# Two-layer hybrid trunk on one core: the first modulation in eight parts of 256 channels in place of four of 512

## The reference, cut to what matters

```python
cond = jax.nn.silu(c)                                   # one row of 2048
for layer in range(DEPTH):
    shift, scale, gate = jnp.split((cond @ w_ada[layer] + b_ada[layer])[:, None, :], 3, axis=-1)
    h = rms_norm(x, norm_g[layer]) * (1.0 + scale) + shift
    (qkv_a, z_a, beta_raw, alpha_raw, glu_in, z_b, q_c, k_c, v_c, z_c,
     q_i, k_i, w_i, gate_raw) = split_columns(h @ w_in[layer])
    ...
    a_half, b_half = jnp.split(glu_in, 2, axis=-1)
    u = causal_depthwise_conv(a_half * jax.nn.sigmoid(b_half), conv_b_w[layer]) + conv_b_b[layer]
    ...
    x = x + gate * (merged @ w_out[layer])
```

## Time and profile before

| | us |
|---|---|
| median of 3 runs | 2204.05 (2202.7 to 2205.69) |
| the profiled execution, its own time | 2206.72 |
| its span in the trace | 2204.9 |
| mean granted TensorE clock | 0.985 |
| PE busy | 2140.4 (97%) |
| POOL busy | 1664.8 (76%) |
| DVE busy | 1225.2 (56%) |

### The profile page before, as it was taken

The page is one execution under the profiler, slowest core; times in us unless marked ns, Lnnn a source line. Parts: engine busy times, 40 slices in busy tenths (PEclk is TensorE's granted clock), DMA queues, the critical chain, the costliest instruction groups (busy, mean ns, idle before and its releaser), DMA issues.

```text
span 2204.9 us, 37807 instructions
## 1 busy us (share of the span) xinstructions
PE 2140.4 (97%) x14842; PEld 1949.9 (88%) x14842; DVE 1225.2 (56%) x2153; ACT 959.7 (44%) x1056; POOL 1664.8 (76%) x676
## 2 busy tenths in 40 slices
PE   5799999999999999999989999999999999999999
PEld 3789999988879988788989999999788998888899
DVE  6859974847655455544562894756667455430110
ACT  3334444483333544444344344446633354444442
POOL 1558858767765898998868886877667679998876
PEclk7889999999999999999999999999999999999999
DMA  9978646545553699898975775555545458966754
GB/s 363 382 266 233 182 126 183 162 138 159 158 157 115 218 353 340 295 340 310 350 256 172 195 211 147 170 163 150 156 148 158 133 182 306 350 206 202 223 192 153
DMA packets 228987, 479.59 MB, mean 218 GB/s; under 512 B 22096, under 2 KB 26448, under 8 KB 220272
## 3 DMA queue, kind: packets, MB, share of 16 engines
q1 hardware_dynamic: 228688, 477.54, 67.1%
q10 hardware_dynamic: 160, 0.13, 0.0%
HBM read 471.19 MB, written 6.29 MB: 217 GB/s over the span
## 4 chain that ended last, share of the span: by engine, by line
PE 42%; POOL 30%; issue 23%; DVE 3%; ACT 1%; DVEq 1%; POOLq 0%; ACTq 0%
POOL wl L539 30%; PE ps L940 13%; PE ps L941 13%; PE ps L942 13%; DVE score L1632 1%; PE ps L1302 0%; ACT wh L560 0%; POOLq L538 0%; PE ps L1309 0%; PE ps L1290 0%; PE ps L1236 0%; ACTq L737 0%; PE ps L1225 0%; PE ps L1258 0%; PE ps L1252 0%
## 5 line engine op out<-in xcount | busy, mean ns | idle before, releaser
L539 POOL TENSOR_TENSOR wl<-raw,wh 128x1024 fp32r<-128x1024 f32 x672 | 1664.6, 2491 | 527.1 <-ACT wh L560 525.4
L560 ACT CAST wh<-raw 128x1024 fp32r<-128x1024 f32 x672 | 703.8, 1050 | 1118.2 <-PE ps L942 871.9
L940 PE MATMUL ps<-ah,wh 128*128 128x256 f32 x3008 | 867.7, 288 | 24.1 <-DVE al L1502 14.9
L941 PE MATMUL ps<-al,wh 128*128 128x256 f32 x3008 | 856.5, 285 | 0.0
L942 PE MATMUL ps<-ah,wl 128*128 128x256 f32 x3008 | 856.1, 285 | 0.0
L940 PEld LDWEIGHTS ps<-ah,wh 128*128 128x128 f32 x3008 | 583.0, 194 | 30.5 <-DVE al L1502 15.2
L941 PEld LDWEIGHTS ps<-al,wh 128*128 128x128 f32 x3008 | 583.2, 194 | 3.9 <-issue 3.6
L942 PEld LDWEIGHTS ps<-ah,wl 128*128 128x128 f32 x3008 | 582.8, 194 | 0.0
L940 PE MATMUL ps<-wh,ah 128*128 128x512 f32 (+1 forms) x832 | 319.8, 384 | 0.9 <-POOL wl L539 0.9
L942 PE MATMUL ps<-wh,al 128*128 128x512 f32 (+1 forms) x832 | 317.1, 381 | 0.0
L941 PE MATMUL ps<-wl,ah 128*128 128x512 f32 (+1 forms) x832 | 317.0, 381 | 0.0
(11 more groups left out here) (280 smaller groups left out, 1702.7 us busy)
## 6 DMA issues: line engine op xcount, KB each, us to landing
raw<-w_in SPq DMA_DIRECT2D x512, 512.0 KB, 3.7
modw<-w_ada SPq DMA_DIRECT2D x64, 1024.0 KB, 7.8
adaw<-w_ada SPq DMA_DIRECT2D x64, 512.0 KB, 8.5
raw<-w_out SPq DMA_DIRECT2D x64, 512.0 KB, 5.2
raw<-w_pc SPq DMA_DIRECT2D x32, 512.0 KB, 3.8
raw<-w_pb SPq DMA_DIRECT2D x32, 512.0 KB, 6.3
raw<-w_pa SPq DMA_DIRECT2D x32, 512.0 KB, 4.8
gbias<-b_gate SPq DMA_DIRECT2D x24, 256.0 KB, 4.3
```

Of the source, the lines that this page charges most:

```text
L539: nc.gpsimd.tensor_tensor(wl[:, s], raw[:, s], wh[:, s].bitcast(F32), ALU.subtract).then_inc(sem("w_split"), 1)
L560: A.copy(wh[:, s], raw[:, s]).then_inc(sem("w_rounded"), 1)
L940: M.matmul(o, lh, rh, start=start, stop=False, skip_group_check=True)
L941: M.matmul(o, lh, rr, start=False, stop=False, skip_group_check=True)
```

## The change

The part is halved: eight parts of 256 channels (`ADA_PARTS`), each still summed over 16 row tiles. A DVE step is now 128x512 and there are 128 in place of 64. A slot still holds 1 MB, but four row tiles of 256 channels, so its DMAs move rows of 1 KB. DVE does four steps of the next part (`ADA_AHEAD`) before it reads the sums. PE uses a part for two channel tiles of the three groups (three chunks), and has the sums of part q + 1 ahead of the third group's piece of part q. SP's and ACT's orders are rewritten to match.

```diff
+        ADA_PARTS = tuple((n, 2) for n in range(0, KT, 2))
+        ADA_AHEAD = (0,) + (4,) * 7
...
+        def by_eighth(slot):
+            return adaw[slot][:].rearrange("p m s n -> p (m s n)").rearrange("p (m s n) -> p m s n", m=4, s=2)
...
@@ SP: ada_load, and the order of both streams
-                    col = part * D + q * GW
-                    sp.dma_start(adaw[j % 4][:, :, part], wa[0, :, 2 * j:2 * j + 2, col:col + GW]
+                    col = part * D + n // 4 * T
+                    sp.dma_start(by_eighth(j % 4)[:, :, part], wa[0, :, 4 * (j % 4):4 * (j % 4) + 4, col:col + T]
                                  ).then_inc(ada_landed[j % 4], 16)
...
                     for n in range(32):
                         ada_load(n)
-                        for i, at in ((5, 10), (4, 9), (3, 7), (2, 6), (1, 4), (0, 2)):
-                            if n >= at and (n - at) % 8 == 0 and n - at < 24:
-                                chunk(6 * ((n - at) // 8) + i)
+                        for i, at in ((2, 5), (1, 3), (0, 2)):
+                            if n >= at and (n - at) % 4 == 0 and n - at < 24:
+                                chunk(3 * ((n - at) // 4) + i)
                     for i in range(18, 24):
                         chunk(i)
...
@@ ACT
-                    for q in range(3):
-                        rounds(hc, RING, hc % RING)
+                    rounds(hc, 3)
+                    for q in range(8):
                         h_high(q)
-                        rounds(hc + RING, 2, (hc + RING) % RING)
-                        hc += 6
-                    rounds(hc, 1, hc % RING)
-                    h_high(3)
-                    rounds(hc + 1, 5, (hc + 1) % RING)
-                    hc += 6
-                    act.wait_ge(sem("w_used"), hc)
-                    A.copy(glt[:], pairv(0)).then_inc(gemm_free[0], 1)
+                        n = 3 if q < 7 else 0
+                        for i in range(n):
+                            rounds(hc + 3 + i, 1, (hc + 3 + i) % RING)
+                        hc += 3
                     rounds(hc, 2)
                     act.wait_ge(sem("w_used"), hc + 2)
+                    A.copy(glt[:], pairv(0)).then_inc(gemm_free[0], 1)
+                    rounds(hc + 2, 1, 2)
+                    act.wait_ge(sem("w_used"), hc + 3)
                     tanh_half(pairv(1), pairv(1)).then_inc(sem("glt_ready"), 1)
-                    rounds(hc + 2, 2, 2)
+                    rounds(hc + 3, 1, 3)
...
@@ PE
-                    for q in range(4):
-                        ada_sum(q)
+                    for q, (k0, k) in enumerate(ADA_PARTS):
+                        if q == 0:
+                            ada_sum(0)
                         for pair in range(3):
-                            part_gemm(hc, pair, H, 4 * q, 4, G_IN, paired=pair == 0)
-                            hc += 2
+                            if q < 7 and pair == 2:
+                                ada_sum(q + 1)
+                            part_gemm(hc, pair, H, k0, k, G_IN, paired=pair == 0)
+                            hc += k // HK
...
@@ DVE: ada_part, and the order of the parts
-                wide, side = ps[:, 6:8, :], acc[:, :, q * GW:(q + 1) * GW]
+                first, width = ADA_PARTS[q]
+                side = acc[:, :, first * P:(first + width) * P]
+                wide = pb[3].rearrange("p (s n) -> p s n", s=2)
...
-                    ahead = ADA_SIDE if q else 0
+                    ahead = 0
...
-                    for q in range(4):
+                    for q, (k0, k) in enumerate(ADA_PARTS):
                         if q == 0:
-                            ada_part(0, 0, 10)
+                            ada_part(0, 0, 12)
                             normed_x()
-                        normed_quarter(q)
-                        ada_part(q, ADA_SIDE + 1 if q else 10, KT)
+                        if q % 2 == 0:
+                            normed_quarter(q // 2)
+                        ada_part(q, ADA_AHEAD[q] + 1 if q else 12, KT)
...
-                        if q < 3:
-                            ada_part(q + 1, 0, ADA_SIDE)
+                        if q < 7:
+                            ada_part(q + 1, 0, ADA_AHEAD[q + 1])
                         quarter_mods(q)
```

More of the change, by code:

```diff
@@ L411, in _ @@
                 if layer == 0:
-                    chunks = [(col, j) for q in range(4) for col in (first, second, first + GW)
-                              for j in range(2 * q, 2 * q + 2)]
+                    chunks = [(col, j) for k0, k in ADA_PARTS for col in (first, second, first + GW)
+                              for j in range(k0 // HK, (k0 + k) // HK)]
                     def chunk(n):
@@ L598, in h_high @@
                     act.wait_ge(sem("gsc_ready"), q + 1)
-                    for kt in range(4 * q, 4 * q + 4):
+                    for kt in range(ADA_PARTS[q][0], sum(ADA_PARTS[q])):
                         last = A.activation(ah[:, kt], merged[:, kt], ACT.Identity, bias=mods[:, kt:kt + 1],
@@ L1027, in ada_sum @@
                 for part in (SHIFT, SCALE):
-                    for j in range(4 * q, 4 * q + 4):
+                    for j in range(ADA_PARTS[q][0], sum(ADA_PARTS[q])):
                         mm = M.matmul(pb[2][:, part * KT + j:part * KT + j + 1], acc[:, part, j * P:(j + 1) * P],
@@ L1415, in ada_part @@
             def ada_part(q, k0, k1):
-                wide, side = ps[:, 6:8, :], acc[:, :, q * GW:(q + 1) * GW]
+                first, width = ADA_PARTS[q]
+                side = acc[:, :, first * P:(first + width) * P]
+                wide = pb[3].rearrange("p (s n) -> p s n", s=2)
                 V.drain()
                 for kt in range(k0, k1):
-                    j, m = kt // 2, kt % 2
+                    j, m = kt // (8 // width), kt % (8 // width)
                     if m == 0:
-                        dve.wait_ge(ada_landed[j % 4], 32 * ((8 * q + j) // 4 + 1))
-                    w = adaw[j % 4][:, m]
-                    ahead = ADA_SIDE if q else 0
+                        dve.wait_ge(ada_landed[j % 4], 32 * ((first * 2 + j) // 4 + 1))
+                    w = by_eighth(j)[:, m]
+                    ahead = 0
                     o = wide if ahead <= kt < KT - 1 else side
@@ L1430, in ada_part @@
                                                    ALU.mult, ALU.add)
-                    if m:
+                    if m == 8 // width - 1:
                         u.then_inc(sem("ada_used"), 1)
@@ L1477, in quarter_mods @@
             def quarter_mods(q):
-                part = slice(4 * q, 4 * q + 4)
+                k0, k = ADA_PARTS[q]
                 dve.wait_ge(sem("ada_turned"), q + 1)
                 for n in (SHIFT, SCALE):
-                    at = n * KT + 4 * q
-                    last = V.tensor_tensor(mods[:, at:at + 4], pb[2][:, at:at + 4], p_(0, "b_ada", at, 4), ALU.add)
-                if q == 3:
+                    at = n * KT + k0
+                    last = V.tensor_tensor(mods[:, at:at + k], pb[2][:, at:at + k], p_(0, "b_ada", at, k), ALU.add)
+                if q == 7:
                     last.then_inc(sem("mods_ready"), 1)
                 V.drain()
-                V.scalar_tensor_tensor(gsc[:, part], mods[:, KT + 4 * q:KT + 4 * q + 4], 1.0,
-                                       p_(0, "norm_g", 4 * q, 4), ALU.add, ALU.mult)
+                V.scalar_tensor_tensor(gsc[:, k0:k0 + k], mods[:, KT + k0:KT + k0 + k], 1.0,
+                                       p_(0, "norm_g", k0, k), ALU.add, ALU.mult)
                 done("gsc_ready")
@@ L1521, in _ @@
                             dve.wait_ge(sem("con_landed"), 16)
-                        if q < 3:
-                            ada_part(q + 1, 0, ADA_SIDE)
+                        if q < 7:
+                            ada_part(q + 1, 0, ADA_AHEAD[q + 1])
                         quarter_mods(q)
-                        for kt in range(4 * q, 4 * q + 4):
+                        for kt in range(k0, k0 + k):
                             V.tensor_scalar(xs[:, kt], merged[:, kt], gsc[:, kt:kt + 1], mods[:, kt:kt + 1],
@@ L1528, in _ @@
                         V.drain()
-                        h_low(2 * q)
-                        h_low(2 * q + 1)
-                        if q < 3:
-                            ada_part(q + 1, ADA_SIDE, ADA_SIDE + 1)
+                        for n in range(k0 // 2, (k0 + k) // 2):
+                            h_low(n)
+                        if q < 7:
+                            ada_part(q + 1, ADA_AHEAD[q + 1], ADA_AHEAD[q + 1] + 1)
                 def products(n):
```

## The result

| | before | after |
|---|---|---|
| median of 4 runs each, same chip | 2204.87 us | 2228.97 us (2226.43 to 2232.2) |
| ratio to before, with its 95% interval | | 1.0111 [1.0096, 1.0125] |
| span of the profiled execution | 2204.9 us | 2224.6 us (its own time 2226.43) |

The change makes the kernel 24.1 us slower; 2225.0 was forecast, range 2215 to 2233.

The account below looks back on a forecast made before the run. PE bounds the kernel: 97% busy, continuous from chunk 24, so delays there reach the end. T(0) 39.6 plus six parts of 16.8 gives T(6) 140.4; plus 35.5, chunk 24 at 175.9 against 155.3: +20.6, 2225 us, range 2215 to 2233.

Parts of the forecast that it names:

- DVE's added steps: DVE in the first modulation: 128 short steps in place of 64 cost 19.6 us more for the same data.
- the stall at part 6: DVE waits about 7 us for ACT's activations, queued behind roundings of chunks 18 to 20, which SP loads late.
- the end of the chain: PE behind T(7): sums 1.0, chunk 20 2.9, chunks 21 to 23 8.6 us, then chunk 24 starts at 175.9.
- Step of 128x512, 0.756 and 0.084 between two: DVE's halved multiply step: 0.756 us, plus a drain of 0.084, 0.84 together.
- T(0) = 39.6: End of DVE's totals of part 0: 38.6 us plus 1.0 for slots ahead of x landing late.
- A part, 16.5 and 0.3 for DMA: Spacing of DVE's totals in the front: 16.5 us of DVE work plus 0.3 for late landings, 16.8 a part.
- T(6): End of DVE's totals of part 6, the seventh of eight: forecast at 140.4 us.
- DMA binds: Rival in the front: 1 KB rows fall to 300 GB/s or less, adding 8 us, 2233 us; chance 0.14.
- T(7): End of DVE's totals of part 7, the last: forecast 22.9 us behind T(6).
- One for one to the end: From chunk 24 on PE is full, so its later start, +20.6 us, passes unchanged into the kernel's end.
- What the change gives back: PE behind the last totals: three chunks in place of six, 8.6 us, already contained in the +20.6.

Follow-up runs that it names:

- Experiment 5: Kernel before with each DVE step of 128x1024 cut into two of 128x512, each with its drain; 2219.61 us, ratio 1.0042.
- experiment 6: Kernel before with each w_ada slot load made as two loads of 256 columns, in 1 KB rows; 2214.19 us, ratio 1.0028.
- experiment 8: Kernel before with only its last 512 channels split into two parts of 256, chunks 18 to 20 loaded between the last slots; 2201.68 us, ratio 0.9971.
- experiment 1: Kernel after with ACT computing part 6's activations ahead of the roundings of chunks 18 to 20; 2228.1 us, ratio to the kernel before 1.0094.
- experiment 2: Kernel after with SP loading chunks 18 to 20 between the slot loads, ahead of the last two; 2230.61 us, ratio to the kernel before 1.0095.
- experiment 7: Kernel after with chunks 18 to 20 loaded early and PE's sums of part 7 behind chunk 20; 2223.91 us, ratio to the kernel before 1.0066.
- experiment 3: Kernel after with PE's sums of each part back at that part's start; 2232.8 us, ratio to the kernel before 1.0117.

## Why the prediction was right

The total, 2225 against 2229, is right by its mechanism: DVE's added steps, the stall at part 6 by the orders of SP and ACT, and the shift that passes on are all there, with sizes near those forecast. One term, the end of the chain, was too small, and it is partly luck that the total hides it. By its steps:

- **Step of 128x512, 0.756 and 0.084 between two:** 0.755 and 0.083. Experiment 5 shows the same in the kernel before, and that 64 doubled steps alone cost 9 to 12 us once the waits for DMA that they hide are taken off.
- **The Trainium skill, "VectorE: DVE Perf Modes"**, section "The TRN2 errata — SBUF-src ops pay a fixed extra latency per instruction": the runs agree with its direction. Whoever takes its 512 elements, the size from which this amortizes, to mean that such steps are free would forecast no loss from them; the kernel paid 0.29 us for each step cut down to that size.
- **T(0) = 39.6:** 38.5. The late landing that I allowed for the slots ahead of `x` did not come.
- **A part, 16.5 and 0.3 for DMA:** T(0) to T(6) took 103.0, 17.2 a part, against 100.8. The 0.3 for DMA were not needed, so six parts of 16.5, 99.0, have to be compared. The 4.0 of difference lie outside the terms: 2.0 in one product at 95.42, which took 3.25 us and not 1.23, 0.8 in `gsc` of 0.52, 0.44 and 0.32 us in place of 0.16 (see the last section for both), and 0.9 in two short idle times that the profile puts to issue (0.50 at 42.5 and 0.43 at 140.7). Without these a part took 15.9 us, and 17.2 with a product, against 15.8 and 17.1 in the working. T(6) = 141.47 against 140.4; that it came so near is helped by the unneeded 0.3 a part.
- **"DMA binds":** it did not. From 36 us on DVE never waited for `adaw`. The sum had its price from the 323 GB/s of the earlier trace rows, a stretch of another load whose packets were 0.86 KB on average (0.97 MB in 1130), and the rival from 300; experiment 6 gives 357 for a mix of 1 KB rows and chunks, 359 where it is at full share. What the Trainium skill states ("DMA: Bandwidth & Descriptors", section "Specifications", line rate from 512 B on) is not borne out either: with nothing changed but the loads, waits for `adaw` rose by 8.3 us. From 359 for the mix and 387 for long rows I estimate about 350 GB/s for the 1 KB rows alone, between the two.
- **The stall at part 6, 7 us:** 7.67, at the place and for the reason given. The last two parts came to T(7) = T(6) + 23.9 against 22.9; 0.7 of it is `al` at 153.99, which took 1.35 and not 0.69 us.
- **The end of the chain:** this term was too small, the one step of the working that failed in size. I had sums 1.0 and chunk 20 2.9 us, at full clock. PE waited 2.76 us for T(7), and the sums took 1.87 us and chunk 20 about 5.1 at the low clock (eight matmuls of `ah`, `wh` 0.64 us apart from 167.21 on). Chunk 24 started at T(7) + 15.5, not + 12.6. I had counted the slow stretch behind the restart at 155.39, and not that the wait for the next totals brings another. With T(6) and T(7) that makes 180.9 against 175.9: 1.1 + 1.0 + 2.9 = 5.0 us.
- **One for one to the end:** 25.5 us at 278 us, 24.0 at 486 to 780 us. The 1.5 us given back and the further drift weren't in the sum. That 5.0 us too few in the front came out as 4 in the total is partly this, and so luck.
- **What the change gives back:** three chunks in place of six behind the last totals, 8.6 us, is there. In eight parts the rest of the change costs 33 us against it. In experiment 8, where DVE's extra steps are 16 and not 64, it pays.

Of the 24 us, by the experiments: DVE's steps are the largest part (doubling their number cost the kernel before 9 to 12 us, experiment 5); the stall is worth 5 to 8 (experiment 1 by its shift, experiment 2 by its shift without the stretched operations; by the medians less shows); the place of the last sums 1.8 (experiment 7 against 2, by the start of chunk 24). They don't add, since each removal uncovers the next wait. No run has the change without all of them, so a part of the 24 us, with the collisions of the last section in it, is not shared out.

## What to carry to other kernels

Splitting work to start a consumer earlier pays at the last piece alone, while the fixed price is paid at every piece: split the tail. Before adding pieces, count the producer's instructions and multiply by their fixed part, read from two sizes of the same operation in the trace; and move the loads that feed the last piece with it, or they stay queued behind the very event that they were to follow at once. After waits of TensorE like those here (2.2 to 8.5 us in the kernel after), price some 3 to 6 us of its next work at the low clock, also where it is the second wait in a row.

## What the runs showed of the hardware

- Short DVE operations grow beside POOL. `merged`, which reads two of the kernel's buffers and no `ps`, took 1.23 us at most places and 3.25 at 95.42 in the kernel after. POOL of the kernel after, at that place and at the earlier `merged` (61.69, 1.23 us):

```profile
61.74 3.44 POOL L545 TENSOR_TENSOR wl<-raw,wh 128x1024 fp32r<-128x1024 f32 x1 [2.96 <-ACT wh L566]
...
95.20 2.40 POOL L545 TENSOR_TENSOR wl<-raw,wh 128x1024 fp32r<-128x1024 f32 x1 [2.59 <-ACT wh L566]
```

  At 95.20 POOL was first: DVE ended 1.07 us after POOL's end. At 61.69 DVE was first by 0.05 us: POOL took 3.44 in place of 2.40, 1.04 more. In experiment 2 `gsc`, two numbers a partition, took 1.45 us from 94.72 and ended at 96.17, and POOL's split ran from 93.78 to 96.16. So whichever starts later stands until the other is nearly or wholly through. Operations with one tensor input grew as well: in the kernel before the first step of part 2 (L1427, 128x1024) took 2.44 us from 72.21, beside a split from 71.76 to 74.10, and 0.75 at 43.61; in experiment 1 two `xs` took 2.66 in place of 0.73. The steps, which read `ps` as one operand, took 0.755 in every part, POOL busy or not. The Trainium skill, "SBUF — State Buffer", section "SBUF: two separate sides", says that VectorE and GpSimd take a shared port pair as an exclusive lock for a whole instruction, among others when the VectorE operation has two inputs in SBUF; the places with two inputs agree. It cost 2.7 us in the kernel after (`merged` and the `al` of 153.99) and another 0.8 in three `gsc`, and 5.4 in experiment 2 (two `merged` and a `gsc`). A finer division has more such operations at times when POOL works, and which of them collide is decided by fractions of a microsecond, so experiment 2 came to T(6) 3.7 us late, and experiment 3 lost 2.8 us between T(0) and T(2), in places that their edits were not meant to touch. No run has the kernel with POOL's splits out of the way.
- PE, which had come back to 0.12 us a matmul by 158.60 (rows of `ah`, `wh` 0.36 us apart), was at 1.2 GHz for the last sums and for nearly all of chunk 20 after a wait of 2.76 us: granted clock 1.00 in 160 to 165 us, 0.52 in 165 to 170. The length of the wait doesn't say at once where the low stretch falls. Behind waits of 2.22 and 3.04 us (55.00 and 88.45) the sums took 1.05 us, at full clock, and the matmuls fell to 0.21 us apart only then, from 55.91 to 59.41 and from 90.19 to 93.59. In experiment 7 the sums behind a wait of 0.47 us took 1.05, and the low stretch came in chunk 21 behind the next wait, of 2.46. Behind waits of 1.28 us (155.30, kernel before) and 1.15 (165.80, experiment 1) none came.
